# FFN gate blocks: T2 added on VectorE in the second product, and T4 on VectorE too in the blocks that a gate block follows

## The reference, cut to what matters

```python
D_FF_2 = 2816
def swiglu(h, w_gate, w_up, w_down):
    return (jax.nn.silu(h @ w_gate) * (h @ w_up)) @ w_down
...
for layer in range(DEPTH):
    x = x + 0.5 * swiglu(rmsnorm(x, norm_ffn1[layer]), ffn1_gate[layer], ffn1_up[layer], ffn1_down[layer])
    x = x + hybrid_mixer(rmsnorm(x, norm_mix[layer]), ...)
    x = x + 0.5 * swiglu(rmsnorm(x, norm_ffn2[layer]), ffn2_gate[layer], ffn2_up[layer], ffn2_down[layer])
return rmsnorm(x, norm_final)
```

## Time and profile before

| of the kernel before | us |
|---|---|
| median of three runs | 3652.09 |
| the profiled execution | 3649.27 |
| its span | 3647.4 |
| TensorE busy (matmul) | 3543.2 |
| VectorE busy | 2513.1 |
| ScalarE busy | 1804.8 |
| GpSimd busy | 285.7 |

### The profile page before, as it was taken

The page is one execution under the profiler, slowest core; times in us unless marked ns, Lnnn a source line. Parts: engine busy times, 40 slices in busy tenths (PEclk is TensorE's granted clock), DMA queues, the critical chain, the costliest instruction groups (busy, mean ns, idle before and its releaser), DMA issues.

```text
span 3647.4 us, 53611 instructions
## 1 busy us (share of the span) xinstructions
PE 3543.2 (97%) x20848; PEld 3028.1 (83%) x20848; DVE 2513.1 (69%) x3210; ACT 1804.8 (49%) x2527; POOL 285.7 (8%) x317
## 2 busy tenths in 40 slices
PE   9999899999999999999999999999999999999999
PEld 7776688888678887989977798999998977789988
DVE  4455666666755767787767577887888676578885
ACT  3335344436633444655555456555655554546554
POOL 0001000000200000100000220000000000310000
PEclk9999999999999999999999999999999999999999
DMA  4000256422005663577621016776777421017774
GB/s 185 36 35 35 92 162 183 140 105 93 24 35 173 173 174 117 172 199 221 176 87 57 12 53 172 201 217 179 204 204 194 133 106 50 2 63 210 207 197 132
DMA packets 70668, 475.18 MB, mean 130 GB/s; under 512 B 7952, under 2 KB 8336, under 8 KB 17552
## 3 DMA queue, kind: packets, MB, share of 16 engines
q1 hardware_dynamic: 46224, 303.97, 23.0%
q0 software_dynamic: 24192, 167.78, 21.0%
HBM read 404.62 MB, written 2.10 MB: 112 GB/s over the span
## 4 chain that ended last, share of the span: by engine, by line
PE 75%; DVE 16%; ACT 5%; DMA 2%; issue 2%; DVEq 0%; POOL 0%; ACTq 0%; SPq 0%; POOLq 0%
PE ps L670 73%; DVE split L2531 6%; ACT arena L1479 3%; DVE arena L2531 3%; PE ps L679 2%; DVE X L2535 2%; ACT split L1479 2%; DMA ring<-in_wts 2%; DVE arena L2535 2%; ACT L1479 1%; DVE arena L3629 0%; DVE ring L2531 0%; DVE small L2547 0%; DVE arena L2527 0%; DVE arena L2559 0%
## 5 line engine op out<-in xcount | busy, mean ns | idle before, releaser
L670 PE MATMUL ps<-split 128*128 128x512 f32 (+1 forms) x16236 | 2955.3, 341 | 51.2 <-DVE arena L2531 14.1
L670 PEld LDWEIGHTS ps<-split 128*128 128x128 f32 x16236 | 2506.9, 191 | 419.3 <-issue 60.3
L2531 DVE TENSOR_TENSOR split<-ring,split 128x1024 fp32r<-128x1024 f32 x674 | 823.0, 1221 | 422.7 <-ACT split L1479 372.6
L1479 ACT ACTIVATE split<-ring 128x1024 fp32r<-128x1024 f32 x674 | 709.7, 1053 | 720.9 <-PE ps L670 660.4
L1479 ACT ACTIVATE arena<-ps 128x512 f32<-128x512 f32 (+5 forms) x656 | 343.0, 523 | 377.1 <-PE ps L670 258.3
L670 PE MATMUL ps<-arena 128*128 128x128 f32 (+9 forms) x3344 | 485.5, 297 | 23.2 <-ACT arena L1479 8.8
L670 PEld LDWEIGHTS ps<-arena 128*128 128x128 f32 (+2 forms) x3344 | 393.8, 190 | 98.0 <-issue 65.6
L1479 ACT ACTIVATE split<-arena 128x1024 fp32r<-128x1024 f32 (+2 forms) x242 | 251.8, 1040 | 211.6 <-PE ps L670 131.4
L2531 DVE TENSOR_TENSOR split<-arena,split 128x1024 fp32r<-128x1024 f32 (+2 forms) x242 | 290.2, 1199 | 79.6 <-ACT split L1479 60.1
L2531 DVE TENSOR_TENSOR arena<-arena 128x512 f32<-128x512 f32 (+7 forms) x302 | 215.2, 713 | 32.7 <-ACT arena L1479 15.7
L2535 DVE SCALAR_TENSOR_TENSOR X<-ps,X 128x512 f32<-128x512 f32 x252 | 174.4, 692 | 69.0 <-PE ps L670 47.5
(11 more groups left out here) (114 smaller groups left out, 1214.2 us busy)
## 6 DMA issues: line engine op xcount, KB each, us to landing
ring<-in_wts SPq DMA_DIRECT2D x260, 1024.0 KB, 5.4
arena<-in_wts POOLq DMA_DIRECT2D x80, 1024.0 KB, 8.4
ring<-ring POOLq DMA_DIRECT2D x28, 1024.0 KB, 9.5
ring<-arena POOLq DMA_DIRECT2D x24, 1024.0 KB, 7.7
ring<-in_wts SPq DMA_DIRECT2D x41, 512.0 KB, 3.5
ring<-in_wts POOLq DMA_DIRECT2D x14, 1024.0 KB, 8.0
arena<-arena POOLq DMA_DIRECT2D x6, 1024.0 KB, 10.3
arena<-in_wts POOLq DMA_DIRECT2D x8, 512.0 KB, 4.5
```

Source lines behind the costliest of these rows:

```text
L670: return e.matmul(out, l, r, start=start, stop=stop, skip_group_check=True)
L1479: o.sig(a.activation(out, i, f, **kw), sig)
L2531: o.sig(v.tensor_tensor(out, a, b, op), sig)
```

## The change

T2 of every gate block is made by VectorE, as T1 plus b22 in b11's slot (`second`). In a wide block other than the first each half follows the split of a T1 piece (r = 1), in the first block both come at r = 2 behind `two`, and in gu..5 it comes at the start of r = 1. T4 of gu..0, gu..2 and gu..4 (the blocks that a gate block follows) is made by VectorE too (`fourth`), at r = 2, in the first block at r = 4. In gu..1, gu..3 and gu..5 T4 stays a DMA, and waits for VectorE's T2. T3 stays. Down blocks stay as they were. The slots of b12 and b22 are now also held until T2 is made. In `whole` f5's low half comes ahead of the sum for f6, and f6's step moves from the end of `first` to the start of r = 3, on VectorE and ScalarE both.

```diff
@@ plan(), block()
-            for q, b, added in (("b11", "t2", "f_t4"), ("b12", "t1", None), ("b22", "b22", None), ("b21", "t4", None)):
-                B.loads[q].end, B.loads[q].added = ("lo", end[b]), added and (added, B.count)
+            downs += 16 * (not B.gated)
+            for pc in next(of for (what, _, _), of in zip(B.order, B.of) if what == "P6"):
+                seconds += B.gated
+                pc.sum = ("f_two", seconds) if B.gated else ("f_t2", downs)
+            B.two = pc.sum
+            B.fourth = name[0:2] == "gu" and name[-1] in "024"
+            fours += 16 * (not B.fourth)
+            for pc in B.of[6]:
+                fourths += B.fourth
+                pc.sum = ("f_four", fourths) if B.fourth else ("f_t4", fours)
+            four = pc.sum
+            for q, b, added in (("b11", "t2", four), ("b12", "t1", None), ("b22", "b22", None), ("b21", "t4", None)):
+                B.loads[q].end, B.loads[q].added = ("lo", end[b]), added
+            if B.gated:
+                B.loads["b12"].added = B.loads["b22"].added = B.two
@@ scalar_program(), ffn()
             next(extra)
             split(next(below))
-            next(extra)
             split(next(below))
...
+                if U.first and r > 2:
+                    next(extra, None)
@@ vector_program()
+    def second(U, q):
+        r = {b: K.RING[:, ld.slot, :] for b, ld in U.loads.items()}
+        v.wait_ge(S[f"ring{U.loads['b22'].slot}"], U.loads["b22"].landed)
+        p = U.of[2][q]
+        c = slice(p.q * U.w, (p.q + p.c) * U.w)
+        tt(r["b11"][:, c], r["b12"][:, c], r["b22"][:, c], ALU.add, "f_two")
+
+    def fourth(U, q):
+        b11, b21 = (K.RING[:, U.loads[b].slot, :] for b in ("b11", "b21"))
+        p = U.of[6][q]
+        c = slice(p.q * U.w, (p.q + p.c) * U.w)
+        tt(b21[:, c], b21[:, c], b11[:, c], ALU.add, "f_four")
@@ whole()
                 if g == 0:
+                    lo("f5", F.shape, 1)
                     tt(F.sixth, F.shape, F.a11, ALU.subtract, "h_sum")
-                    lo("f5", F.shape, 1)
@@ gate_up()
                 if r == 2:
                     two(U)
+                    if U.first:
+                        second(U, 0)
+                        second(U, 1)
+                if r == 1 and not wide:
+                    second(U, 0)
+                if U.first and r > 2:
+                    next(extra, None)
...
+                    if r == 1 and wide:
+                        second(U, y)
+                    if U.fourth and r == (4 if U.first else 2):
+                        fourth(U, y)
@@ pool_program(), block()
-        if U.first:
-            g.wait_ge(S["f_two"], begun)
-            g.dma_start(at["b11"], b22, accum_op=ALU.add).then_inc(S["f_t2"], 16)
-            g.wait_ge(S["used"], U.begin)
...
+        g.wait_ge(*((S["used"], U.begin) if U.first else (S["lo"], U.before.split["t3"])))
+        g.dma_start(t3, b22).then_inc(S["f_base"], 16)
+        g.wait_ge(S["f_base"], U.count)
+        g.dma_start(t3, b12, accum_op=ALU.add).then_inc(S["f_t3"], 16)
+        if not U.gated:
             g.wait_ge(S["lo"], U.split["b11"])
             g.wait_ge(S["f_t1"], U.of[2][-1].sum[1])
             g.wait_ge(S["f_t3"], U.count)
             g.dma_start(at["b11"], t3, accum_op=ALU.add).then_inc(S["f_t2"], 16)
+        if U.fourth:
+            return
         g.wait_ge(S["lo"], U.split["b21"])
-        g.wait_ge(S["f_t2"], U.count)
+        g.wait_ge(S[U.two[0]], U.two[1])
         g.dma_start(at["b21"], at["b11"], accum_op=ALU.add).then_inc(S["f_t4"], 16)
```

More of the change, by code:

```diff
@@ L245, in plan @@
     lins, loads, turned, forms, n = {}, [], [], [], 0
-    sums, shapes, before, blocks, summed_up, done, holds = 0, 0, None, 0, 0, 0, {}
+    sums, shapes, before, blocks, summed_up, seconds, downs, fourths, fours, done, holds = 0, 0, None, 0, 0, 0, 0, 0, 0, 0, {}
     slots, held, kept = [0, 1, 2, 3], {}, {}
@@ L373, in ffn @@
     def ffn(l, n_):
-        nonlocal n, blocks, summed_up, shapes, done
+        nonlocal n, blocks, summed_up, seconds, downs, fourths, fours, shapes, done
         key, new, us = f"fgu{n_}_{l}", [], []
@@ L405, in block @@
         def block(name, key, p, h, kbase, c1, c2, w, at=None):
-            nonlocal blocks, summed_up
+            nonlocal blocks, summed_up, seconds, downs, fourths, fours
             blocks += 1
@@ L3882, in pool_program @@
     Y, M = K.y, K.m
-    F, begun = K.f, 0
-    def opened(U):
-        nonlocal begun
-        begun += 16
-        g.wait_ge(S["lo"], U.split["b11"])
-        g.wait_ge(S["f_t1"], U.of[2][-1].sum[1])
-        ld = U.loads["b11"]
-        g.dma_start(K.RING[:, ld.slot, 0:U.h * U.w], W["wts"][U.loads["b12"].i], accum_op=ALU.add).then_inc(S["f_two"], 16)
+    F = K.f
     def block(U):
@@ L3900, in block @@
         t3 = (F.t3first if U.first else F.t3)[:, 0:n]
-        if U.first:
-            g.wait_ge(S["f_two"], begun)
-            g.dma_start(at["b11"], b22, accum_op=ALU.add).then_inc(S["f_t2"], 16)
-            g.wait_ge(S["used"], U.begin)
-            g.dma_start(t3, b22).then_inc(S["f_base"], 16)
-            g.wait_ge(S["f_base"], U.count)
-            g.dma_start(t3, b12, accum_op=ALU.add).then_inc(S["f_t3"], 16)
-        else:
-            g.wait_ge(S["lo"], U.before.split["t3"])
-            g.dma_start(t3, b22).then_inc(S["f_base"], 16)
-            g.wait_ge(S["f_base"], U.count)
-            g.dma_start(t3, b12, accum_op=ALU.add).then_inc(S["f_t3"], 16)
+        g.wait_ge(*((S["used"], U.begin) if U.first else (S["lo"], U.before.split["t3"])))
[3 more added lines that the diff above has]
+        if not U.gated:
             g.wait_ge(S["lo"], U.split["b11"])
@@ L4016, in pool_program @@
         g.tensor_tensor(r1[:, j:j + 1], r1[:, j:j + 1], E.power, ALU.pow).then_inc(S["fx_r"], 1)
-        if j == 1:
-            opened(lins["ffn10"][0])
     for l in range(2):
-        if l:
-            opened(lins["ffn11"][0])
         for U in lins[f"ffn1{l}"]:
@@ L4060, in pool_program @@
             lower(t)
-        opened(lins[f"ffn2{l}"][0])
         for U in lins[f"ffn2{l}"]:
@@ L4089 @@
            "ml_e", "ml_m", "ml_y", "ml_v", "ml_r", "ml_b", "ml_z", "power", "e_blk", "c_s", "c_e", "c_p", "n_m", "ln_x", "relu", "pt", "ple_x", "cq", "lat", "qrope", "qirope",
-           "ix_s", "ix_a", "isc", "gp", "madd", "a_m", "m_v", "od_a", "od_d", "xn", "again1", "again2", "t1", "t2", "t3", "t4", "fx_lo", "f_t1", "f_t2", "f_t3", "f_t4", "f_base", "f_two", "h_sum", "h_hi", "h_form", "early", "silu_u", "u", "shape", "fhi", "form", "part", "jn_a", "jn_d", "fx_s", "fx_m", "fx_r", "hc", "cv", "hi_v", "hp_a", "hp_d", "rw_a", "rw_d", "hv_a", "hv_d", "gp_a", "gp_d", "lr_a", "lr_d", "lru", "grow", "h67", "st", "kd", "hd", "he", "xl",
+           "ix_s", "ix_a", "isc", "gp", "madd", "a_m", "m_v", "od_a", "od_d", "xn", "again1", "again2", "t1", "t2", "t3", "t4", "fx_lo", "f_t1", "f_t2", "f_t3", "f_t4", "f_base", "f_two", "f_four", "h_sum", "h_hi", "h_form", "early", "silu_u", "u", "shape", "fhi", "form", "part", "jn_a", "jn_d", "fx_s", "fx_m", "fx_r", "hc", "cv", "hi_v", "hp_a", "hp_d", "rw_a", "rw_d", "hv_a", "hv_d", "gp_a", "gp_d", "lr_a", "lr_d", "lru", "grow", "h67", "st", "kd", "hd", "he", "xl",
            "oh", "sq", "bbr", "s0x", "s1", "kw", "xi", "xd", "gz", "gn_a", "gn_d", "ct", "state", "og_t", "og", "done", "out"]
```

## The result

The kernel after takes 3680.71 us, the median of four runs (3677.12 to 3681.74); the kernel before beside it 3651.49 us (four runs, 3649.52 to 3656.58). The ratio is 1.0076, with a 95% interval of 1.0059 to 1.0094: about 28 us slower, where 10 us were forecast, and above the whole range of the prediction (3643 to 3678). The profiled execution of after took 3677.12 us and its span is 3675.3 us, 27.9 us longer than that of before.

The account below looks back on a forecast made before the run. TensorE was taken as the bound, busy for 3543.2 of 3647.4 us. The terms +17.9 + 8.8 - 16.4 = +10.3 us gave 3659.6 on the profiled execution and 3662 for the median, range 3643 to 3678.

Parts of the forecast that it names:

- the credit of 16.4 us for the holes before N4: In gu..1 and gu..3, earlier T4 DMAs close the 3 us holes: 10.2 us gained, plus 6.2 of clock.
- T2 in gu..5: One VectorE addition replaces an accumulation that holds nothing up: 0, within 1 us per FFN either way.
- The first block: In gu..0, four additions on a VectorE without idle time delay N4: 4.1 + 3 x 4.6 = +17.9 us.
- T2 in wide blocks other than the first: In gu..1 and gu..3, two additions make TensorE stand 1.1 us before N3: eight blocks, +8.8 us.
- T4 in gu..2 and gu..4: T4 additions are among the four that VectorE's idle time takes up there: 0, at most 0.5 us a block.
- that fall was covered: In first blocks, a clock fall at P6 is covered by the hole before N4.
- slower still: Uncovered clock falls in first blocks (6.4 us) and b12 late in three blocks (8 us): 3676 us, chance 0.12.
- The rival of late loads: SP's queue late, so down blocks' T1 is late: eight 3 us holes instead of three, +15, 3667 us, chance 0.05.
- The slow clock behind the holes: Behind the three 3 us holes before N4, granted clocks of 0.64, 0.80 and 0.79 over 8 us cost 6.2 us.

Follow-up runs that it names:

- before_again: The kernel before, unchanged, profiled once more; 3645.22 us, ratio 0.9991 to before.
- first_back: The kernel after with the first block of each FFN back as before: T2 and T4 by DMA, old order of f5 and f6; 3660.38 us, ratio 1.0037.
- first_old_order: The kernel after with the first block's T2 and T4 still on VectorE, but f5, f6 and f7 in the old order and places; 3677.28 us, ratio 1.0081.
- f5_order: The kernel before with only f5's low half made ahead of the sum for f6 in each first block; 3649.16 us, ratio 0.9994.
- gu5_back: The kernel after with T2 of gu..5 back as a DMA on GpSimd's queue; 3667.02 us, ratio 1.0058 to before.
- t4_gu5_dve: The kernel after with T4 of gu..5 on VectorE as well; 3672.31 us, ratio 1.0067 to before.
- form_late: The kernel after with the down block's a11 form and f7's difference made at the end of r = 2 instead of r = 1; 3675.57 us, ratio 1.0075.
- no_t4_first: The kernel after with T4 of the first block back as a DMA accumulation on GpSimd's queue; 3680.33 us, ratio 1.0085 to before.

## Why the prediction was wrong

The direction was right, and so was the sign of each step that had one. The size was not: +10.3 us were worked out against the profiled execution of before, and the two spans differ by 27.9. Two steps failed: the credit of 16.4 us for the holes before N4, and T2 in gu..5 at 0. By step:

| step of the prediction | forecast | against the first execution | against before_again |
|---|---|---|---|
| The first block | +17.9 | +15.3 | +17.7 |
| T2 in wide blocks other than the first | +8.8 | +11.0 | +11.0 |
| The holes before N4 in those blocks | -16.4 | -9.1 | -2.7 |
| T4 in gu..2 and gu..4 | 0 | 0 | 0 |
| T2 in gu..5 | 0 | +7.2 | +7.2 |
| the rest of the program | 0 | +3.5 | +1.8 |
| sum | +10.3 | +27.9 | +35.0 |

The row of the N3 holes is eight times what N3 takes longer, 7.13 for 5.76 us from signal to signal; the row of the N4 holes is what is left of the pairs' difference (1.9 - 11.0 and 8.3 - 11.0).

*The first block* was right. The hole before P6 is 3.33 us (forecast 3.3), the one before N4 2.17 (forecast 2.3), and N4 is 7.85 us later (1542.02 for 1534.17), of which the block's start gives 3.8 (its previous block ends at 1498.71 for 1494.95). So +4.1 us, the forecast number. gu210 and gu200 paid 2.8 to 2.9 us for the 4.6 I took, gu110 5.5. In gu200 and gu210 the execution of before had a slow clock behind the hole before N3 (N3 took 9.40 and 9.25 us from signal to signal), which before_again had not (7.48 and 8.19); against before_again the four paid 4.1, 4.4, 5.5 and 3.7. first_back and first_old_order show that it is the additions. The clock did fall behind the hole before P6 in three of the four, as in this window of after, with a granted clock of 0.80, the lower level of 1.2 GHz for part of it:

```profile
2612.22:2620.22 8.00, 8.00 (x55) 8.00 (x56) 7.19 (x6) 5.15 (x6) 0.00 (x0) 0.80 0.35 144
```

The 96 matmuls take 13.1 to 13.2 us there for 11.75, and the hole before N4 is shorter by 1.1 to 1.5 (1.10, 0.80 and 0.71 us, for 2.17). So that fall was covered, as the prediction said, and did not cost 1.6 us each as in the rival "slower still". The measured time lies nearest to that rival's 3676, but not by its mechanism: the falls were covered, and VectorE waited for b12 0.3 to 1.4 us in five of the eight blocks, for 3.4 to 4.7 at the three holes of before. The rival of late loads was priced wrongly on record: eight holes in the place of three are 15 us, but without the credit, and with the 17.9 and 8.8 us that come anyhow, that is 3652 + 15 + 26.7 = 3694 and not 3667. It did not come either.

*T2 in wide blocks other than the first* was the right mechanism with a term a quarter too small: 1.37 us per block for 1.1. I gave VectorE 0.8 us in hand, from 1556.83 to 1557.6, and 0.1 for the signal. The piece's delay was exactly 1.77; TensorE's need was nearer than I had it: a product takes 5.76 us from signal to signal, not the 5.86 that I read from merged rows. The hole itself is 1.12 us, as forecast.

*The holes before N4* is the step that failed first. Its mechanics came out as worked out: with the shift of 7.85 us taken off, T4's DMA goes out at 1553.6 (forecast 1553.1) and the load that T1 waits for at 1559.9 (forecast 1560.0). SP's timeline and GpSimd's of after:

```profile
1561.47 0.86 POOL L3944 DMA_DIRECT2D ring<-ring  x1 [19.02 <-DVE ring L2545]
...
1567.80 0.33 SPq L4102 DMA_DIRECT2D ring<-in_wts  x1
```

The load is 6.3 us behind and lands after 7.4 (forecast 7.2), and the hole is 0.19 us. In all eight blocks of after T4's DMA goes out 13.4 us after the block's start and the load 19.7, so the distance is 6.3 us everywhere: that part of the mechanism held. But I took the three holes of one execution for what before has in each. In before_again two of the three are absent. What the change can save there is what before has on average, and the three executions with its transfers (before, before_again, f5_order) have 12.8, 6.4 and 6.6 us of such holes, mean 8.6. Moreover after has 656.5 - 641.8 - 11.0 = 3.7 us of excess left, since its load, 1.8 us later, still lands too late in four blocks; the six kernels with its additions in gu..1 and gu..3 and the form at its old place have 1.4 to 3.7, mean 2.5. The credit is thus some 8.6 - 2.5 = 6 us, an estimate from nine executions, not 16. The slow clock behind the holes, 6.2 of my 16.4 us, was the weakest part of it: it did not come at all behind the 1.81 and 2.52 us holes of before_again.

*T2 in gu..5* is the other step that failed, at "an accumulation that holds nothing up now". The accumulation held nothing up, but with the addition in its place the next load waits for T2 too, where it waited only for the split of T1, and it goes out at one moment with T4's DMA. I had asked for the two queues in gu101, seen that 0.5 us between a load and a T4 DMA makes the second of them land late, and not asked it in gu..5, where the same diff puts b12's next load and T4 on one signal. Both ways out, gu5_back and t4_gu5_dve, give back 6 to 7.2 us in the blocks.

With the means of all executions that have the same code in the blocks in question, the parts are: first block 200.4 - 183.1 = +17.3, holes before N3 +11.0, holes before N4 -6, gu..5 91.6 - 85.0 = +6.6, in all +29, beside 28 by the ratio. Of the 18 us that the forecast missed, 10 are the credit and 7 gu..5. The medians agree as far as they go: undoing the first block is worth 1.0076 - 1.0037 = 0.0039, gu..5 0.0018, gu..1 and gu..3 0.0020, in all 0.0077 of before's time; but only the first of these is clear of the intervals, so that the sum fits as well as this is luck. What stays open: between executions the rest of the program differs by up to 14 us in these traces, and the 3.5 us of the rest in the first comparison are not shown to be the change's, since nothing was changed there; which runs have them I can't tell from one profile each. Why the copy of T3 takes 5 us in one block and 8 in another of the same program is not shown either.

## What to carry to other kernels

A hole that the change is to close counts only with a second execution of the kernel before: a hole that is in one and not in the other hangs on a time that varies, here that of T4's DMA. Ask what sets it, look at all places of the kind (eight per execution here), and credit an average, not a row. Where one signal is made to release two transfers on two queues, look for who needs the second of them, in every stage that the edit touches, the small ones too. On an engine that is busy for 77% of a stage, ask for the idle time at the very place (0.99 us between two splits), not for its share: what is added where there is none comes out on the bounding engine for the most part, 4.1 us of the 5.3 of four additions. And when a wait is taken away, look at which transfer then goes out earlier, and beside what: form_late lost at N4 what it gained at N3.

## What the runs showed of the hardware that was not expected

- How long a transfer takes beside another hangs on which goes out first and by how much. A 1 MB weight load took 8.3 to 12.2 us when it went out 0.3 to 2.1 us behind T4's accumulation of 1 MB (13 blocks), 6.5 to 7.7 us when 0.17 us behind it to 0.23 us ahead (3), and 5.8 to 8.1 us when 3.6 us or more behind (32; the table of before_again). The distance alone is no rule: in form_late, 3.7 us behind, it took 9.3 to 10.8 us. T4's accumulation of 512 KB in gu..5 took 4.9 to 7.1 us when issued 1.3 to 2.4 us behind a load and 8.3 to 9.6 us when 0.5 us behind one (after). One of 1 MB took 13.2 to 15.0 us in the first blocks of no_t4_first.
- A slower clock came behind each of the 3.0 us holes of before and in three of four FFNs behind the 3.33 us hole of after, in gu100 not: P6 took 11.75 us there after a hole as long. Among the shorter holes it came behind 1.91 and 1.77 us before N3 in gu200 and gu210 of before (granted clock 0.79 over the next 8 us), and not behind 2.52 us in gu213 of before_again (1.00). One row of a fall is no rule for the next.
